# Sliding attention and the filters of the long convolutions in one block, in a two-layer mixer kernel on one Trainium2 core

## The chip, the core and the metric

The kernel is one program on one core of a Trainium2 chip. The metric is the device time of a launch in microseconds, the median of several runs. All arithmetic is 32-bit floating point. The engines are named as the profile names them: PE (TensorE; PEld is its weight load), DVE (VectorE), ACT (ScalarE), POOL (GpSimd), SP (SyncE, which issues most DMAs). "mem" is the on-chip memory, "banks" are the eight PSUM banks of 512 words per partition.

## What is computed

Two layers over 512 tokens of width 1024, with 256 context tokens. The first layer mixes by a gated delta rule and a differential attention; the second, which the change touches, by a sliding-window attention (8 heads of 64, two key heads, blocks of 128 queries against up to three blocks of keys and the 256 context tokens) and by two long convolutions with learned filters:

```python
def mixer_cd(hx, hz, w_in, w_out, sink, hy_conv, ...):
    qx, kx, vx, ux = split_cols(hx @ w_in, CD_SPLITS)
    qx = rope2d(...); kx = rope2d(...)
    ocx = swa_latent(qx, kx, vx, kz, vz, sink)
    odx = hyena(ux, hy_conv, hyena_filters(n, hy_w1, ...), hy_bias)
    out_x = jnp.concatenate([ocx, odx], axis=-1) @ w_out

def hyena_filters(n, w1, b1, w2, b2, w3, freq):
    h = jnp.sin(freq[0] * (feats @ w1 + b1))
    h = jnp.sin(freq[1] * (h @ w2 + b2))
    h = (h @ w3).reshape(n, 2, 2, 512) * jnp.exp(-t * deltas)
    kern = concatenate([h[:, :, 0], zeros, flip(h[1:, :, 1])])
    kern = kern * rsqrt(sum(kern * kern, axis=0) + EPS)
    return rfft(kern)

def hyena(u, conv_w, kf, bias):
    v, x1, x2 = jnp.split(dwconv(u, conv_w), 3, axis=-1)
    z = v
    for o, gate in enumerate((x1, x2)):
        z = gate * (fft_long_conv(z, kf[:, o]) + z * bias[o])
    return z
```

Each layer ends with an output projection, a norm and a feed-forward part.

## The kernel before, in words

The program is a row of stages. A stage is one block with a hand-written order of instructions for each engine; semaphores order them inside the block, and the next block begins when all engines have left this one. Weights come in slices of 1 MB or less through a ring of four buffers (`Core.stream`, `prefetch`, `issue`); SP issues a slice when its buffer has been read.

The stages around the change, in order:

- `down_and_project` (L1914): the down projection of the first feed-forward part; beside it POOL issues, one after the other, 24 slices of `w_mod` (`Down.load_side`, L1796) which PE multiplies after every second unit (L304); then the projections `swa_q` (4 tiles), `hy_in` (12 tiles, a three-tap convolution on ACT and DVE), `swa_k`, and the values. A tile is eight matmuls of 128x512 (L1865). At its end SP also loads the four slices of `cd_out`, the weights of the output projection after the mixing.
- `window_attention` (L2583): 32 units (4 query blocks x 8 heads). For a unit PE makes scores on one half of its rows (L2620, L2621, L2623), DVE adds window masks (L2691, L2693), takes the maximum (L2694) and forms the bias of the exponential (L2697), ACT takes the exponential (L2667) and that of the sink (L2669), DVE sums, inverts and scales (L2704 to L2706), PE turns the probabilities (L2633), ACT keeps them (L2660), and for two heads at once PE multiplies with the values (L2645), which DVE copies out (L2712). A score area is 512 or 640 wide, and there are two of them. POOL does nothing.
- `hyena` (L2991), a row of blocks: `turn_tiles` (L2747) turns eight tiles to token order; `filter_features` (L2783) loads all tables and makes the two sine layers; then for each of the two orders `filter_lags` (L2838: 8 products with `w3`, decay on DVE, squares on ACT summed over all tokens by PE with a matrix of ones, L2853), `transform` (L2902) of the filter with a scaling by the norm (L3014), `transform` of the signal with the complex product, shared between DVE (`product_c`, `join_s`) and POOL (`product_s`, L3033 to L3037), and `inverse` (L2960). After the first order four tiles are turned back. A transform is 16 matmuls of 128x512 (L2918), each two records in the trace; DVE unfolds its halves (L2931, L2932).
- `mix_and_up` (L1391: output projection), and the rest of the feed-forward part.

## Time and profile before

| | |
|---|---|
| median of 3 runs | 2686.13 us (2685.66 to 2688.75) |
| the profiled execution's own time | 2678.73 us |
| its span, first to last instruction | 2676.9 us |
| PE busy / DVE / ACT / POOL | 89% / 34% / 20% / 9% |
| granted PE clock, mean | 0.953 |

The profile is of one execution, read on its one core. Times in its rows are microseconds from the start of the span unless marked ns. A share of busy time is an average over stages that have different limits, so what counts for a stage is which chain of waits ends last in it. PEclk is the granted clock of PE as a share of 2.4 GHz.

### The profile page before, as it was taken

What the parts mean: (1) busy time and instruction counts of PE and PEld (TensorE: products, weight loads), DVE (VectorE), ACT (ScalarE), POOL (GpSimd) and SP (SyncE); (2) the same over time, 40 slices, a digit from 0 to 9 for tenths busy, and PEclk for the clock granted to TensorE, in tenths of its full rate; (3) what the DMA queues carried; (4) which work ended last, traced back from release to release, by engine and by line L of the source; (5) the groups of instructions that cost most, each with busy time, mean ns of one, the idle gap of its engine ahead of it and who ended that gap; (6) DMA issues with size and microseconds to landing.
All of it is one profiled execution on the core that took longest, in us unless ns stands there. A gap on an engine that the chain in (4) does not pass through costs nothing. (4 is left out here: it accounts for less than half of the span.)

```text
span 2676.9 us, 37700 instructions
## 1 busy us (share of the span) xinstructions
PE 2390.0 (89%) x16488; PEld 1631.4 (61%) x16488; DVE 899.2 (34%) x1717; ACT 537.4 (20%) x1252; POOL 232.4 (9%) x293
## 2 busy tenths in 40 slices
PE   4999899779958999999999999998667599999998
PEld 2566555468856755555569997456423385444798
DVE  2225602277732322222210032317555533222111
ACT  2104601421203311111110021115311031111110
POOL 1000100047720000000000000000020200000000
PEclk9999899889988999999999999998888799999999
DMA  8340010000030111111115566120100011221354
GB/s 304 132 158 26 1 47 16 0 2 4 4 128 1 63 39 56 63 32 63 53 58 164 164 192 207 48 77 2 60 0 0 0 63 63 71 86 63 97 144 139
DMA packets 190785, 193.46 MB, mean 72 GB/s; under 512 B 4970, under 2 KB 174622, under 8 KB 190430
## 3 DMA queue, kind: packets, MB, share of 16 engines
q1 hardware_dynamic: 177950, 145.55, 17.9%
q0 software_dynamic: 11584, 42.24, 4.4%
q8 instruction: 130, 2.13, 0.3%
q10 hardware_dynamic: 1088, 3.26, 0.3%
q14 instruction: 33, 0.27, 0.0%
HBM read 188.94 MB, written 2.10 MB: 71 GB/s over the span
## 5 line engine op out<-in xcount | busy, mean ns | idle before, releaser
L1446 PE MATMUL banks<-mem 128*128 128x512 f32 x1312 | 618.1, 591 | 0.0
L1780 PE MATMUL banks<-mem 128*128 128x128 f32 x3520 | 404.3, 277 | 11.2 <-PEq L1369 9.9
L1780 PEld LDWEIGHTS banks<-mem 128*128 128x128 f32 x3520 | 399.7, 193 | 21.2 <-issue 19.9
L461 DVE SCALAR_TENSOR_TENSOR mem<-banks,mem 128x511 f32<-128x511 f32 (+1 forms) x168 | 106.1, 660 | 748.5 <-ACT mem L1517 325.3
L1446 PEld LDWEIGHTS banks<-mem 128*128 128x128 f32 x1312 | 247.8, 189 | 172.0 <-issue 153.2
L1449 PEld LDWEIGHTS banks<-mem 128*128 128x128 f32 x672 | 127.1, 189 | 161.9 <-issue 161.9
L1449 PE MATMUL banks<-mem 128*128 128x256 f32 x672 | 200.1, 378 | 0.0
L1865 PE MATMUL banks<-mem 128*128 128x512 f32 x400 | 188.6, 602 | 6.0 <-issue 6.0
L1515 ACT ACTIVATE mem<-banks,mem 128x512 f32<-128x512 f32 x88 | 60.6, 689 | 628.3 <-PE banks L1449 373.5
L1391 PE MATMUL banks<-mem 128*128 128x256 f32 x640 | 144.4, 386 | 13.3 <-PEq L715 11.1
L917 PE MATMUL banks<-mem 64*64 64x64 f32 x3840 | 128.8, 221 | 18.5 <-DVE mem L1193 11.4
L1391 PEld LDWEIGHTS banks<-mem 128*128 128x128 f32 x640 | 123.3, 194 | 32.5 <-issue 14.0
L917 PEld LDWEIGHTS banks<-mem 64*64 64x64 f32 x3840 | 121.2, 137 | 28.7 <-DVE mem L1193 13.7
L398 PE MATMUL banks<-mem 128*128 128x512 f32 x256 | 130.9, 592 | 2.5 <-PEq L514 1.2
L1807 DVE COPY mem<-banks 128x128 f32<-128x128 f32 x40 | 11.7, 293 | 351.0 <-PE banks L1780 350.9
L1865 PEld LDWEIGHTS banks<-mem 128*128 128x128 f32 x400 | 75.3, 191 | 74.4 <-issue 70.8
L465 DVE SCALAR_TENSOR_TENSOR mem<-banks,mem 128x511 f32<-128x511 f32 (+1 forms) x168 | 105.8, 658 | 4.0
L1796 POOL DMA_DIRECT2D mem<-in_w_mod x24 | 17.3, 723 | 856.1 <-POOLq L1369 610.8
L401 PEld LDWEIGHTS banks<-mem 128*128 128x128 f32 x256 | 48.4, 189 | 61.7 <-issue 61.7
L1801 ACT ACTIVATE mem<-banks 128x128 f32<-128x128 f32 x40 | 11.1, 278 | 361.1 <-PE banks L1780 349.0
L2918 PE MATMUL banks<-mem 128*128 128x512 f32 x128 | 62.8, 653 | 17.0 <-PEq L2843 6.1
L401 PE MATMUL banks<-mem 128*128 128x256 f32 x256 | 76.2, 378 | 0.0
(306 smaller groups left out, 2641.0 us busy)
## 6 DMA issues: line engine op xcount, KB each, us to landing
mem<-in_ffn_w_up SPq DMA_DIRECT2D x44, 1024.0 KB, 5.4
mem<-in_ffn_w_down SPq DMA_DIRECT2D x64, 704.0 KB, 6.5
mem<-in_w_mod POOLq DMA_DIRECT2D x40, 1024.0 KB, 7.5
mem<-in_ab_w_in SPq DMA_DIRECT2D x14, 1024.0 KB, 5.3
mem<-in_w_mod SPq DMA_DIRECT2D x8, 1024.0 KB, 14.8
mem<-in_cd_w_in SPq DMA_DIRECT2D x8, 1024.0 KB, 5.3
mem<-in_ab_w_out SPq DMA_DIRECT2D x4, 1024.0 KB, 9.2
mem<-in_cd_w_out SPq DMA_DIRECT2D x4, 1024.0 KB, 5.1
```

What stands on the lines that cost most here:

```text
L398: last = nc.tensor.matmul(c.ps[:, 2 * (n % slots), :], w[:, k, :], ht[:, k, 0:N_X], start=k == 0, stop=k == KT - 1)
L401: last = nc.tensor.matmul(c.ps[:, 2 * (n % slots) + 1, 0:z], w[:, k, :], ht[:, k, N_X:N_X + z], start=k == 0, stop=k == KT - 1)
L461: step = v.scalar_tensor_tensor(out[:, 1:n], src[:, 0:n - 1], tap(0), out[:, 1:n], ALU.mult, ALU.add)
L465: step = v.scalar_tensor_tensor(out[:, 0:n - 1], src[:, 1:n], tap(2), out[:, 0:n - 1], ALU.mult, ALU.add)
L917: last = mm(c.ps[pa, LEVEL[i], fr], lhs[pa, fr], rhs[pa, fr], start=True, stop=True)
L1391: last = nc.tensor.matmul(c.ps[:, unit_banks[n % 4], 0:256], src[:, k, t * 128:(t + 1) * 128], w[:, k, :], start=k == 0, stop=k == KT - 1)
L1446: last = nc.tensor.matmul(c.ps[:, bank, :], w[:, k, :], ht[:, k, 0:N_X], start=k == 0, stop=k == KT - 1)
L1449: last = nc.tensor.matmul(c.ps[:, bank + 1, 0:z], w[:, k, :], ht[:, k, N_X:N_ALL], start=k == 0, stop=k == KT - 1)
L1515: f(dst[:, 0:N_X], c.ps[:, bank, :], ACT.Identity, scale=middle_tap(n, half)).then_inc(drained, 1)
L1780: last = c.nc.tensor.matmul(c.ps[:, n % self.n_banks, 0:128], hidden[:, k, t * 128:(t + 1) * 128], w, start=k == 0, stop=k == FT - 1)
L1865: last = c.nc.tensor.matmul(c.ps[:, self.bank(n)[0], :], w[:, k, :], ht[:, k, 0:N_X], start=k == 0, stop=k == KT - 1)
L2918: last = nc.tensor.matmul(c.ps[:, 4 * f + 2 * s + odd, :], hy.fwd[:, s, 2 * odd + t, f * 128:(f + 1) * 128], src(s)[:, 2 * odd + t, :], st ...
```

## The change

It does five things.

1. `down_and_project` also makes the filter features (the two sine layers) in its `hy_in` part: POOL issues six small loads ahead of the `w_mod` slices, PE makes one 33- and one 64-row matmul after tiles 5 and 8, DVE six operations after each, ACT one sine after each. Its SP no longer loads `cd_out`; that is now done by the convolution block once the last spectrum is formed.
2. Attention goes by pairs of heads: the scores of the two heads of a pair are issued in turns on the two row halves of PE, into one pair of score areas; two turns and one product with values for a pair. DVE does both maxima, then both weighings, of a pair.
3. In the same block all filter work is done in 16 steps, one for each pair: for each order four steps of lags (two products, kept by ACT, decayed, combined and accumulated by POOL with six operations, squared by ACT) and four steps of transform (four matmuls, kept by ACT, unfolded by POOL with two operations). The sum over tokens is taken once for each order at the end, from sums that POOL accumulated. Tables are loaded by SP at the start of the block.
4. The filters are no longer scaled by their norm; the norm is applied after the inverse transforms.
5. Turning, both convolutions and both gates are one block, `convolutions`; the inverse is in two halves, and the first half of it may run while DVE is at the second half of the product.

```diff
-        for n in range(self.issued, min(hi + ahead, len(self.loads))):
+        for n in range(self.issued, min(hi + ahead, self.range_of["cd_out"][0] if hi < self.range_of["cd_out"][1] else len(self.loads))):
...
+    net = FilterFeatures(c, Hyena(c), sem, 7)
...
-                c.stream(sp, name)
+                c.stream(sp, name, 0 if name == "swa_v" else RING)
...
+            net.load(pool)
             down.load_side(pool)
...
+                if n in (5, 8):
+                    net.multiply(pe, (n - 5) // 3)
...
+                if n in (6, 9):
+                    net.sine(act, (n - 6) // 3)
...
+                if n in (5, 8):
+                    net.reduce(dve, (n - 5) // 3)
...
+class Filters:
...
+    def load(self, eng):
+        hy, a = self.hy, self.c.a
+        eng.dma_start(hy.w3, a["hy_w3"][0]).then_inc(self.came, 16)
+        eng.dma_start(hy.decay, a["t_decay"].rearrange("(t p) n -> p t n", p=128)).then_inc(self.came, 16)
+        for s in range(2):
+            eng.dma_start(hy.fwd[:, s], a["t_fwd"][s].rearrange("(t p) n -> p t n", p=128)).then_inc(self.came, 16)
+        eng.dma_start(hy.bias0, a["hy_bias"][0, 0].partition_broadcast(128)).then_inc(self.came, 16)
...
+    def multiply(self, pe, n, part):
...
+        if n == 0 and part == 0:
+            pe.wait_ge(self.came, self.LOADED)
+        if n:
+            pe.wait_ge(self.kept, 2 * (n - 1) + part + 1)
+        if lag:
+            t, col = n % 8, (order * 2 + part) * 512
+            last = c.nc.tensor.matmul(out, hy.h2[:, t * 128:(t + 1) * 128], hy.w3[:, col:col + 512], start=True, stop=True)
+        else:
+            f, s = (n % 8 - 4) // 2, n % 2
+            if (f, s, part) == (0, 0, 0):
+                pe.wait_ge(self.ready, 8 * (order + 1))
+            for t in range(2):
+                last = c.nc.tensor.matmul(out, hy.fwd[:, s, 2 * part + t, f * 128:(f + 1) * 128],
+                                          hy.lags[:, s, 2 * part + t, :], start=t == 0, stop=t == 1)
...
+    def keep(self, act, n):
...
+        for part in range(2):
+            act.wait_ge(self.product, 2 * n + part + 1)
+            if n >= 2 and part == 0:
+                self.after(act, n - 2)
...
+    def after(self, eng, n):
...
+        if lag:
+            eng.wait_ge(self.ready, 2 * (lags + 1))
+            eng.wait_ge(self.squared, 2 * (lags + 1))
+        else:
+            eng.wait_ge(self.unfolded, 2 * (4 * (n // 8) + n % 8 - 4 + 1))
+    def square(self, act, n):
+        lags, lag = self.lag_step(n)
+        if lag:
+            for part in range(2):
+                act.wait_ge(self.decayed, 2 * lags + part + 1)
+                if lags:
+                    act.wait_ge(self.added, 2 * (lags - 1) + part + 1)
+                self.c.nc.scalar.activation(self.hy.lag_sq[part], self.hy.lag_raw[2 * (n % 2) + part], ACT.Square)\
+                    .then_inc(self.squared, 1)
+    def weigh(self, pool, n):
...
+            raw = [hy.lag_raw[2 * (n % 2) + part] for part in range(2)]
+            for part in range(2):
+                pool.wait_ge(self.kept, 2 * n + part + 1)
+                g.tensor_tensor(raw[part], raw[part], hy.decay[:, t, :], ALU.mult).then_inc(self.decayed, 1)
+            pool.wait_ge(self.decayed, 2 * lags + 2)
+            if order and t == 0:
+                pool.wait_ge(self.product, 16)
+            g.tensor_tensor(hy.lags[:, 0, t, :], raw[0], raw[1], ALU.add).then_inc(self.ready, 1)
+            g.tensor_tensor(hy.lags[:, 1, t, :], raw[0], raw[1], ALU.subtract).then_inc(self.ready, 1)
+            for part in range(2):
+                pool.wait_ge(self.squared, 2 * lags + part + 1)
+                if part or t:
+                    pool.wait_ge(self.added, 2 * lags + part)
+                    ins = g.tensor_tensor(hy.acc[order], hy.acc[order], hy.lag_sq[part], ALU.add)
+                else:
+                    ins = g.tensor_copy(hy.acc[order], hy.lag_sq[part])
+                ins.then_inc(self.added, 1)
+        else:
+            f, s = (n % 8 - 4) // 2, n % 2
+            total, mirrored, odd = hy.kern[order][:, s, f], hy.kern[order][:, s, 2 + f], hy.lag_raw[2 * (n % 2) + 1]
+            pool.wait_ge(self.kept, 2 * n + 2)
+            g.tensor_tensor(mirrored, *((odd, total) if s else (total, odd)), ALU.subtract).then_inc(self.unfolded, 1)
+            pool.wait_ge(self.unfolded, 2 * (4 * order + n % 8 - 4) + 1)
+            g.tensor_tensor(total, total, odd, ALU.add).then_inc(self.unfolded, 1)
...
+            def scores(p):
+                q, hp = pairs[p]
+                if p:
+                    pe.wait_ge(exped, 2 * p)
...
+                for hh, k0, k1, at in parts:
+                    pa = slice(64 * hh, 64 * hh + 64)
...
+            for i in range(n_pairs + 2):
+                if i < n_pairs:
+                    scores(i)
+                if 0 <= i - 2:
+                    values(i - 2)
+                if 0 <= i - 1 < n_pairs:
+                    turn_unit(2 * i - 2)
+                    filters.multiply(pe, i - 1, 0)
+                    turn_unit(2 * i - 1)
+                    filters.multiply(pe, i - 1, 1)
+            filters.norm_multiply(pe)
...
+            for i in range(n_pairs + 2):
+                if 0 <= i - 2:
+                    filters.keep(act, i - 2)
+                if 0 <= i - 3:
+                    filters.square(act, i - 3)
+                if 0 <= i - 1 < n_pairs:
+                    turned_copy(2 * i - 2)
+                if i < n_pairs:
+                    exps(2 * i)
+                    exps(2 * i + 1)
+                if 0 <= i - 1 < n_pairs:
+                    turned_copy(2 * i - 1)
...
+            for i in range(n_pairs + 2):
+                if i < n_pairs:
+                    maximum(2 * i)
+                    maximum(2 * i + 1)
+                    weigh(2 * i)
+                    weigh(2 * i + 1)
...
+def convolutions(c):
...
+            sp.wait_ge(spec_done, 4)
+            c.prefetch(sp, "cd_out")
...
+            for order in range(2):
+                forward(order, 0)
+                if order == 0:
+                    pe.wait_ge(v_act, 4)
+                    pe.wait_ge(v_dve, 4)
+                forward(order, 1)
+                if order == 0:
+                    pe.wait_ge(back_in, 32)
+                backward(order, 0)
+                if order:
+                    pe.wait_ge(unfolded, 8)
+                    for k in range(4):
+                        for t in range(4):
+                            last = nc.tensor.transpose(c.ps[:, bank(1, 1) + k, t * 128:(t + 1) * 128], hy.v[:, t, k * 128:(k + 1) * 128],
+                                                       c.tab["ident"])
+                        last.then_inc(z_turned, 1)
+                backward(order, 1)
...
+            def multiply(order, f):
+                g = 2 * order + f
+                kern = lambda s, mirror: hy.kern[order][:, s, 2 * mirror + f, :]
+                for s in range(2):
+                    dve.wait_ge(product, 4 * g + 2 + s + 1)
+                    dve.wait_ge(even_out, 2 * g + s + 1)
+                    total, mirrored, odd = z(s, 0), z(s, 1), c.ps[:, bank(order, f) + 2 * s + 1, :]
+                    v.tensor_tensor(mirrored, *((odd, total) if s else (total, odd)), ALU.subtract)
+                    v.tensor_tensor(total, total, odd, ALU.add).then_inc(unfolded, 1)
+                dve.wait_ge(unfolded, 2 * g + 2)
+                for mirror, total in enumerate((one, other)):
+                    v.tensor_tensor(total, z(0, mirror), kern(0, mirror), ALU.mult)
+                    link(v.tensor_tensor(part, z(1, mirror), kern(1, mirror), ALU.mult))
+                    link(v.tensor_tensor(total, total, part, ALU.subtract))
+                if order and f == 0:
+                    dve.wait_ge(inverse, 4)
+                v.tensor_tensor(hy.spec[:, 0, f, :], one, other, ALU.add)
+                v.tensor_tensor(hy.spec[:, 0, 2 + f, :], one, other, ALU.subtract).then_inc(spec_c, 1)
+                dve.wait_ge(spec_s, g + 1)
+                link(v.tensor_tensor(other_s, other_s, other_part_s, ALU.add))
+                v.tensor_tensor(hy.spec[:, 1, f, :], one_s, other_s, ALU.subtract)
+                v.tensor_tensor(hy.spec[:, 1, 2 + f, :], one_s, other_s, ALU.add).then_inc(spec_done, 1)
+                dve.wait_ge(spec_done, g + 1)
             for f in range(2):
+                multiply(0, f)
+            for t in range(4):
+                dve.wait_ge(inverse, t + 1)
+                link(v.tensor_tensor(one, c.ps[:, t, :], hy.root0, ALU.mult))
+                dve.wait_ge(weighted, t + 1)
+                link(v.tensor_tensor(one, one, hy.vb[:, t, :], ALU.add))
+                v.tensor_tensor(hy.v[:, t, :], one, hy.x1[:, t, :], ALU.mult).then_inc(gated, 1)
+                dve.wait_ge(gated, t + 1)
             for f in range(2):
+                multiply(1, f)
...
-def window_attention(c):
...
-def hyena(c):
...
-    window_attention(c)
-    hyena(c)
+    attention_and_filters(c)
+    convolutions(c)
```

## Rows read from the trace of the kernel before

**Rows 1.** The page's first line: the span.

```profile
span 2676.9 us, 37700 instructions
```

**Rows 2.** Stretches: us, busy PE, PEld, DVE, ACT, POOL, clock, DMA share, GB/s.

```profile
1803.60:1906.30 102.70, 82.28 (x593) 61.00 (x593) 74.10 (x229) 54.04 (x129) 0.01 (x1) 0.90 0.04 11
1906.30:2135.90 229.60, 144.10 (x340) 67.12 (x340) 126.02 (x162) 33.19 (x49) 35.72 (x24) 0.78 0.06 18
...
1929.70:1953.60 23.90, 20.84 (x32) 7.42 (x33) 10.91 (x16) 8.85 (x12) 0.00 (x0) 0.75 0.00 1
```

**Rows 3.** Timeline, one 640-wide attention unit: start, us, engine, line, operation.

```profile
1872.77 0.30 DVE L2691 TENSOR_TENSOR banks<-banks,mem 128x128 f32<-128x128 f32 x1 [0.69 <-PE banks L2623]
...
1874.55 0.80 ACT L2667 ACTIVATE mem<-banks,mem 128x640 f32<-128x640 f32 x1 [0.38 <-DVE mem L2697]
...
1874.82 0.56 DVE L2706 TENSOR_SCALAR mem<-mem 128x640 f32<-128x640 f32 x1
...
1875.29 0.29 DVE L2712 COPY mem<-banks 128x128 f32<-128x128 f32 x1
1875.34 0.28 ACT L2669 ACTIVATE mem<-mem 128x1 f32<-128x1 f32 x1
```

**Rows 4.** Timeline of PE: first scores, turns, values, scores on two row halves, transforms.

```profile
1810.62 1.23 PE L2620 MATMUL banks<-mem 64*128 64x256 f32 x4 [7.83 <-DVE mem L2681]
...
1863.45 0.77 PE L2633 MATMUL banks<-mem 128*128 128x128 f32 x5 [0.71 <-DVE mem L2706]
...
1864.15 1.32 PE L2645 MATMUL banks<-mem 128*64 128x128 f32 x20
...
251.52 1.89 PE L537 MATMUL banks<-mem 64*128 64x512 f32 x8
...
1954.55 13.06 PE L2918 MATMUL banks<-mem 128*128 128x512 f32 x30
...
1973.60 16.82 PE L2918 MATMUL banks<-mem 128*128 128x512 f32 x32 [5.99 <-PEq L224]
```

**Rows 5.** Four lines of code: duration ns min/median/max, first and last start.

```profile
L1141 POOL TENSOR_TENSOR mem<-mem x12: 1035/1043/1052, 598.0 to 767.6; 128x512 f32<-128x512 f32 x12
...
L3034 POOL TENSOR_TENSOR mem<-mem x4: 1704/1708/1712, 1987.4 to 2106.0; 128x512 f32<-128x512 f32 x4
...
L3014 DVE TENSOR_TENSOR mem<-mem x16: 684/690/695, 1962.8 to 2076.0; 128x512 f32<-128x512 f32 x16
...
L3024 DVE TENSOR_TENSOR mem<-mem x8: 1746/1750/1756, 1986.2 to 2109.8; 128x512 f32<-128x512 f32 x8
```

**Rows 6.** Timeline of the convolutions: turns, table load, product halves, gate, last inverse.

```profile
1906.30 4.08 PE L2760 MATMUL banks<-mem 128*128 128x128 f32 x32 [0.66 <-PEq L2598]
...
1951.19 1.28 ACT L2899 ACT_TABLE_LOAD   x1
...
1984.89 0.68 DVE L2932 TENSOR_TENSOR mem<-mem,banks 128x512 f32<-128x512 f32 x1
...
1997.35 0.69 DVE L3042 TENSOR_TENSOR mem<-mem 128x512 f32<-128x512 f32 x1
...
1998.77 0.69 DVE L2931 TENSOR_TENSOR mem<-mem,banks 128x512 f32<-128x512 f32 x1 [0.74 <-ACT mem L2949]
...
2013.03 0.69 DVE L3042 TENSOR_TENSOR mem<-mem 128x512 f32<-128x512 f32 x1
...
2022.64 0.69 DVE L3047 TENSOR_TENSOR mem<-mem 128x512 f32<-128x512 f32 x1 [1.36 <-PE banks L2977]
...
2116.95 16.87 PE L2979 MATMUL banks<-mem 128*128 128x256 f32 x64 [23.61 <-PEq L2908]
```

**Rows 7.** Timeline at the start of `down_and_project`, and a row of DMA issues.

```profile
1379.46 0.77 POOL L1796 DMA_DIRECT2D mem<-in_w_mod  x1 [610.82 <-POOLq L1369]
...
1392.13 1.04 PE L304 MATMUL banks<-mem 128*2 128x256 f32 x16
...
mem<-in_cd_w_out SPq DMA_DIRECT2D x4, 1024.0 KB, 5.1
```

More of the change, by code:

```diff
@@ new lines, in exps @@
+            def exps(u):
+                p, hh = u // 2, u % 2
+                n = cols(p)
+                act.wait_ge(maxed, 2 * p + 2)
+                if u >= 4:
+                    act.wait_ge(turned_ps, u - 3)
+                    act.wait_ge(weighed, u - 3)
+                nc.scalar.activation(prob[:, u % 4, 0:n], score(p, hh), ACT.Exp, bias=neg[:, u % 4:u % 4 + 1],
+                                     scale=scale, accum_out=total[:, u % 4:u % 4 + 1]).then_inc(exped, 1)
+                h = 2 * pairs[p][1] + hh
+                nc.scalar.activation(sink_exp[:, u % 4:u % 4 + 1], sink[:, h:h + 1], ACT.Exp,
+                                     bias=neg[:, u % 4:u % 4 + 1]).then_inc(sink_exped, 1)
@@ L2672, in _ @@
+            filters.norm(act)
+        @block.gpsimd
+        def _(pool):
+            for n in range(Filters.STEPS):
+                filters.weigh(pool, n)
         @block.vector
@@ new lines, in forward @@
+            def forward(order, f):
+                for odd in range(2):
+                    if f == 0:
+                        if order:
+                            pe.wait_ge(gated, 2 * odd + 2)
+                        else:
+                            pe.wait_ge(v_act, 2)
+                            pe.wait_ge(v_dve, 2)
+                    for s in range(2):
+                        for t in range(2):
+                            last = nc.tensor.matmul(c.ps[:, bank(order, f) + 2 * s + odd, :], hy.fwd[:, s, 2 * odd + t, f * 128:(f + 1) * 128],
+                                                    hy.v[:, 2 * odd + t, :], start=t == 0, stop=t == 1)
+                        last.then_inc(product, 1)
@@ new lines, in backward @@
+            def backward(order, f):
+                pe.wait_ge(spec_done, 2 * order + f + 1)
+                for i in range(4):
+                    cut = slice(i * 128, (i + 1) * 128)
+                    if order == 0:
+                        parts = [(i // 2, f)]
+                    else:
+                        parts = [(0, 1), (1, 0), (1, 1)] if f else [(0, 0)]
+                    for odd, half in parts:
+                        tokens = slice(256 * odd, 256 * odd + 256)
+                        for s in range(2):
+                            table, spec = hy.back[:, s, half, :], hy.spec[:, s, 2 * odd + half, :]
+                            flags = dict(start=(half, s) == (0, 0), stop=(half, s) == (1, 1))
+                            if order == 0:
+                                last = nc.tensor.matmul(c.ps[:, bank(order, 0) + i, :], table[:, cut], spec, **flags)
+                            else:
+                                last = nc.tensor.matmul(c.ps[:, bank(order, 0) + i, tokens], spec[:, cut], table[:, tokens], **flags)
+                    if f:
+                        last.then_inc(inverse, 1)
@@ L2763, in _ @@
         @block.scalar
         def _(act):
[L2765 to L2775 removed]
+            copy = lambda dst, src: nc.scalar.activation(dst, src, ACT.Copy)
@@ new lines, in _ @@
+            for n in range(0, 8, 2):
+                act.wait_ge(turned, n + 1)
+                copy((hy.v, hy.x1)[n // 4][:, n % 4, :], c.ps[:, n, :]).then_inc(v_act, 1)
+            for order in range(2):
+                for f in range(2):
+                    g = 2 * order + f
+                    if g:
+                        act.wait_ge(spec_c, g)
+                        act.wait_ge(spec_s, g)
+                    for s in range(2):
+                        act.wait_ge(product, 4 * g + s + 1)
+                        copy(z(s, 0), c.ps[:, bank(order, f) + 2 * s, :]).then_inc(even_out, 1)
@@ L2902, in transform @@
-def transform(c, src, hy, values, finish, finish_pool=None, join=None):
-    nc = c.nc
-    st, sem = stage(c)
-    with st, nc.Block() as block:
-        product, chained, pool_chained = sem("product"), sem("chained"), sem("pool_chained")
-        even_out, unfolded, finished, pool_finished = sem("even_out"), sem("unfolded"), sem("finished"), sem("pool_finished")
-        @block.tensor
-        def _(pe):
-            for f in range(2):
-                for s in range(2):
-                    for odd in range(2):
-                        for t in range(2):
-                            last = nc.tensor.matmul(c.ps[:, 4 * f + 2 * s + odd, :],
-                                                    hy.fwd[:, s, 2 * odd + t, f * 128:(f + 1) * 128],
-                                                    src(s)[:, 2 * odd + t, :], start=t == 0, stop=t == 1)
-                    last.then_inc(product, 1)
+            link = chain(pool, pool_chained)
```

610 lines of the change are left out of this document (258 added, 352 removed).

## The prediction

> **What bounds the kernel now.** I read the profiled execution's span first [rows 1], then the stretches of the two stages that the change rewrites [rows 2], then their timelines [rows 3, 4, 6]. Its own time is 2678.7 us, 7.4 us below the median of the runs; the sum is made on it and put on the median at the end. Attention takes 102.7 us, from 1803.6 to 1906.3, the convolutions 229.6 us, to 2135.9 [rows 2]. Neither is at the pace of a full engine: in the convolutions PE is busy for 144.1 us and DVE for 126.0, one after the other, and the granted clock is 0.78. There PE waits for DVE: each half of a complex product takes DVE 15 us (first unfold of the second half at 1998.77, last join at 2013.03 + 0.69 [rows 6]), and PE restarts at the low one of its two clocks (1.2 and 2.4 GHz). A transform of 32 records takes 30 in 13.06 us, 0.435 each, when warm, and 32 in 16.82 from cold: 2.8 us more [rows 4]. In attention it is the chain scores, maximum, exponential, weighing, turn, with PE busy for 82.3 of 102.7 us, and POOL idle.
>
> **Projection: +2.7 us.** Two matmuls of 512 columns in a stretch where PE is full: 2 x 2 x 0.435 = 1.7. DVE's six operations and ACT's sine lie beside the next tile (8 matmuls, 7 us), with a table load. POOL issues six small loads ahead of the first `w_mod` slice. Bounds: nothing, or 6 x 0.77 = 4.6, since PE first needs a slice at 1392.13, 12.7 us after its issue [rows 7]; I take 1. SP no longer moves `cd_out` here.
>
> **Convolutions: 229.6 becomes 103.** What goes: the features, the lags of both orders (23.9 for the first [rows 2]) and the filter's transforms. What stays, as a chain from the block's start:
> - turns 4.1 [rows 6]; the first forward transform, 8 matmuls at 0.87 and a few at the low clock: 13.5; unfolding then ends at 15.0. The rest of a half takes 1997.35 + 0.69 - 1985.57 = 12.5 [rows 6]: 27.5;
> - the second half, 15.0 with the copies of ACT beside DVE: 42.5. The second forward and the first inverse half lie under it;
> - the inverse's second half: first tile after 2 matmuls at the low clock, 3.5, then four gates of three chained operations like L3047's 0.69, 2.2 each: 55.0. This was 8 matmuls more per order, then a block of turns;
> - the half of a forward transform that waits for the last gate, 1.7 and unfold: 59.8; + 12.5 + 15.0 = 87.3. The turns of z lie under it;
> - the last inverse: 24 of the former 32 matmuls. 32 took 16.87 [rows 6], 8 warm ones fewer take 3.4 less: 101; two DVE operations and the block's end: 103.
> The `cd_out` slices are issued at 87.3 and land 5.1 us later in the quiet median [rows 7]; PE needs the first at 103, the fourth some 20 us after. Cost nothing under that cover of 16 us; without it up to 5 us.
> Gain 126.6. Bounds: 95 (no cold restarts, ACT and DVE steps overlap better) and 112 (each of the four waits costs one more restart of 2.8).
>
> **Attention with the filter steps: 102.7 becomes 158.** This is the uncertain term. Terms for a pair:
> - PE: scores on two row halves. L537 does that for 2 x 768 columns in a span of 1.89 us, where at 0.87 for 512 columns they would take 2.6 one after the other [rows 4]; by columns 2 x 640 is 1.5, 2 x 512 1.15. Values 1.32, turns 2 x 0.66 [rows 4], lag matmuls 2 x 0.87, transform matmuls 4 x 0.87. With gaps: transform step 8.1 us (640 wide) or 7.3 (512).
> - DVE: a unit takes 1875.29 - 1872.77 = 2.5 [rows 3], a pair with its copy 5.25, and DVE now waits between maxima and weighings for ACT's first exponential and sink, 1874.55 to 1875.62 [rows 3], 1.2 with hops: 6.5, or 5.4 at 512.
> - POOL: six operations of 512 in a lag step, two in a transform step. Alone one takes 1.04 us (L1141); beside DVE's operations with two inputs from mem 1.71 (L3034), and DVE's own go from 0.69 (L3014) to 1.75 (L3024) [rows 5]: the sum of both durations. DVE's weighing has such an operation (L2704) and L2706, whose 0.56 for 640 elements [rows 3] is quicker than L3014's 0.69 for 512, so it uses more than one path; no row shows it beside POOL. Its bounds are no wait and 1.04. I take 1.2 us a unit for both: a lag pair on DVE is 8.6 at 640 and 7.7 at 512. POOL loses 1.5 to DVE: 8.0 for six.
> The Trainium skill, "SBUF — State Buffer", section "Who interferes with whom", says that the shared port pair is locked for a whole instruction, two-input operations and `tensor_scalar` in its two-port mode among them. The trace agrees for two inputs; L2704 and L2706 would each wait up to one POOL operation.
>
> Order of time from the stage's start. First scores at 1810.62 - 1803.6 = 7.0, as before [rows 4]. PE ends pair 0's turns and first lag step at 20.6, at the low clock. Lags 1 to 3 run at 7.8, 7.8, 8.3: 44.5. Then PE's queue meets `ready`, the wait that the change adds: transform step 4 needs all four lags. POOL gets the last pair of lags only after ACT's keep, and before them the two additions for the step before, which wait for ACT's squares: 1.7 + 6 x 1.04 + contention 1 = 9 us after PE began pair 5: 53.5; behind that wait stand the turn of the pair's second head and so everything. The rest of that pair 4.5 + 1 cold, three transform pairs 24.3: 83.3. Pair 9 at 7.3 and lags of order two at 8.6, 8.6, 8.0: 115.8. The second wait 9: 124.8; 5.5; two pairs 14.6; the last without scores 6: 151. The sum of squares, `Ln`, a table load of 1.28 [rows 6] and `Exp`, with the last unfolding: 6.5. In all 157.5, +55.
> Bounds: no contention, lag steps at 6.9 and 5.8 (the chain score-maximum-exponential), the two waits 8: 143, +40. Every POOL operation at 1.71: lag step 10.5, the waits 12.5: 178, +75.
>
> **Sum.** -126.6 + 55 + 2.7 = -69: 2678.7 becomes 2610, and 2617 on the scale of the median.
>
> **The rivals.**
> 1. Light contention: attention +40, total 2602. For it: L1141's 12 runs, over 170 us of another stage, are all within 1.035 and 1.052 [rows 5], though DVE worked there too. Against: L3034's 1.71. 0.22.
> 2. Full contention, every POOL operation at 1.71 and DVE held for a whole one at each of its own: attention +75, total 2638. For it: rows 5, where both ran densely. Against: of a unit's eight DVE operations only L2704 and L2706 are of that sort, the others have an input in PSUM or one element. 0.20. That is what the Trainium skill's lock rule (same page and section) gives if POOL is never idle; the trace shows it only for equal lengths.
> 3. The scores of the two heads run one after the other, 2.1 instead of 1.5, and PE, not DVE, is the bound in all pairs: 16 x 0.6 + 6 = +16, total 2633. Against: L537's 1.89. 0.08.
> 4. Slower than before: in-order queues leave nothing of a filter step beside its pair. PE's product n waits for ACT's keep n-1, ACT's square for POOL's decay, POOL's addition for ACT's square. A lag step then costs 6.9 + 1.7 + ACT's four operations of 512, each under L2667's 0.80, 2.5 + 6 x 1.71 = 21.4, a transform step 8.1 + 1.7 + 3.4 = 13: 8 x 21.4 + 8 x 13 + 14 = 289, +187, total about 2750. It decides from an attention stage above 226 us. Against: each wait looks back one or two steps, and two kept areas alternate. 0.02.
> 5. A better overlap than forecast of both stages (convolutions 95, attention +35): 2588. 0.06.
>
> **How the numbers follow.** The forecast has 0.42. The time is its own, 2617. The range takes in rivals 1 to 3 and the bounds of the convolutions: low 2617 - 15 - 8 - 9 = 2585, high 2638 + 9 + 3 = 2650. A difference of 0.2% (5 us) is about what a measurement of this kernel can tell. All cases but rival 4 are far beyond it: faster 0.97, same 0.01, slower 0.02.
>
> **What would show it.** In the profile after: a stretch of attention of some 158 us with POOL busy for over 70, the scaling longer than L2706's 0.56 when POOL runs, PE idle twice for about 5 us behind POOL at the first transform matmul of each order; convolutions of 103 us in four product halves of 15; DMA not on the chain at the output projection. Wrong would be: lag pairs no slower than transform pairs (rival 1), POOL operations all near 1.7 (rival 2), score matmuls of 2 us a pair (rival 3).

## The result and the profile after

The changed kernel takes 2606.26 us, the median of 4 runs (2604.04 to 2607.28); the kernel before, beside it on the same chip, 2687.28 (2685.66 to 2688.75). The ratio is 0.9698, interval [0.9681, 0.9714]: 81 us faster, where 69 were forecast (2617). The profiled execution took 2604.04 us.

The page, then the two rewritten stretches (us, busy PE, PEld, DVE, ACT, POOL, clock, DMA share, GB/s), which answer to [rows 1, 2]:

```profile
span 2602.2 us, 37620 instructions
...
1808.30:1961.70 153.40, 120.70 (x698) 73.12 (x699) 91.17 (x229) 79.91 (x183) 79.80 (x64) 0.84 0.07 20
1961.70:2063.20 101.50, 71.76 (x209) 41.34 (x209) 75.55 (x84) 9.39 (x16) 38.48 (x24) 0.85 0.16 52
```

| | before | after | change | forecast |
|---|---|---|---|---|
| projection ends at | 1803.6 | 1808.3 | +4.7 | +2.7 |
| attention (after: with all filter work) | 102.7 | 153.4 | +50.7 | +55 |
| convolutions | 229.6 | 101.5 | -128.1 | -126.6 |
| the rest of the span | 541.0 | 539.0 | -2.0 | 0 |
| span | 2676.9 | 2602.2 | -74.7 | -69 |

The other 6 us of the 81 stand in no stage of these two traces: before's profiled execution lay 8.6 us under the median given here, after's 2.2 under its own.

The timeline of PE in attention (start, us, engine, line): a lag pair of 512 columns, the two waits for POOL, and three scores of transform pairs with 640 columns:

```profile
1833.82 1.13 PE L2870 MATMUL banks<-mem 64*128 64x256 f32 x8
...
1839.27 1.39 PE L2870 MATMUL banks<-mem 64*128 64x128 f32 x12
...
1860.87 3.75 PE L2723 MATMUL banks<-mem 128*128 128x512 f32 x4 [4.08 <-POOL mem L2782]
...
1867.83 1.36 PE L2870 MATMUL banks<-mem 64*128 64x256 f32 x12
...
1875.06 1.36 PE L2870 MATMUL banks<-mem 64*128 64x256 f32 x12
...
1882.33 1.36 PE L2870 MATMUL banks<-mem 64*128 64x256 f32 x12
...
1930.60 3.75 PE L2723 MATMUL banks<-mem 128*128 128x512 f32 x4 [6.39 <-POOL mem L2782]
```

The first such wait ended 52.6 us after the stage's start (forecast 53.5), the second 122.3 (124.8), and what was left took 31.1 (32.7). A transform pair takes 7.2 us, not 8.1.

What single DVE and POOL operations take in the same stage (ns minimum/median/maximum): the addition of the sink's exponential, the scaling, the negated maximum, the reciprocal, POOL's decay:

```profile
L2979 DVE TENSOR_TENSOR mem<-mem x32: 146/159/1220, 1819.3 to 1948.9; 128x1 f32<-128x1 f32 x32
...
L2981 DVE TENSOR_SCALAR mem<-mem x32: 486/556/1452, 1819.7 to 1949.3; 128x512 f32<-128x512 f32 x16, 128x640 f32<-128x640 f32 x16
...
L2974 DVE TENSOR_SCALAR mem<-mem x32: 214/214/216, 1816.9 to 1946.8; 128x1 f32<-128x1 f32 x32
...
L2980 DVE RECIPROCAL mem<-mem x32: 162/164/167, 1819.5 to 1949.1; 128x1 f32<-128x1 f32 x32
...
L2777 POOL TENSOR_TENSOR mem<-mem x16: 1258/1270/1280, 1827.6 to 1926.6; 128x512 f32<-128x512 f32 x16
```

An addition of one element for each partition takes up to 1.22 us, about one POOL operation long. The scaling is held in the same way, the other two never. Here is how it looks in the pair that begins at 1839.27 (DVE and POOL take turns, then PE has waited 3.06 us for DVE):

```profile
1839.49 1.26 DVE L2981 TENSOR_SCALAR mem<-mem 128x512 f32<-128x512 f32 x1
1840.55 1.32 POOL L2781 TENSOR_TENSOR mem<-mem 128x512 f32<-128x512 f32 x1
1840.67 1.22 DVE L2979 TENSOR_TENSOR mem<-mem 128x1 f32<-128x1 f32 x1
1841.84 1.25 POOL L2782 TENSOR_TENSOR mem<-mem 128x512 f32<-128x512 f32 x1
...
1842.13 1.26 DVE L2981 TENSOR_SCALAR mem<-mem 128x512 f32<-128x512 f32 x1
...
1843.73 1.97 PE L2895 MATMUL banks<-mem 128*64 128x128 f32 x16 [3.06 <-DVE mem L2998]
```

Over the whole stage the groups of these two lines show it (busy us, mean ns):

```profile
L2981 DVE TENSOR_SCALAR mem<-mem 128x512 f32<-128x512 f32 (+1 forms) x32 | 23.8, 745 | 1.1
L2979 DVE TENSOR_TENSOR mem<-mem 128x1 f32<-128x1 f32 x32 | 13.5, 422 | 19.8 <-ACT mem L2925 19.7
```

### The profile page after: what moved, and what is told of

Its sections match the earlier page's. It is cut to its first block and busy times, and to the rows that moved or that the text cites. A ratio compares the mean times of both kernels' runs of the same rounds, so it can differ in the third digit from the quotient of the medians.

```text
span 2602.2 us, 37620 instructions
## 1 busy us (share of the span) xinstructions
PE 2358.5 (91%) x16466; PEld 1618.3 (62%) x16466; DVE 871.6 (33%) x1651; ACT 542.5 (21%) x1276; POOL 318.3 (12%) x363
## 3 DMA queue, kind: packets, MB, share of 16 engines
q10 hardware_dynamic: 1088, 3.26, 0.3%
## 5 line engine op out<-in xcount | busy, mean ns | idle before, releaser
L1446 PE MATMUL banks<-mem 128*128 128x512 f32 x1312 | 618.1, 591 | 0.0
L1865 PE MATMUL banks<-mem 128*128 128x512 f32 x400 | 191.4, 609 | 6.0 <-issue 6.0
L917 PE MATMUL banks<-mem 64*64 64x64 f32 x3840 | 128.0, 221 | 18.6 <-DVE mem L1193 11.4
L398 PE MATMUL banks<-mem 128*128 128x512 f32 x256 | 130.9, 592 | 2.5 <-PEq L514 1.2
L304 PE MATMUL banks<-mem 128*2 128x256 f32 x768 | 54.9, 413 | 23.5 <-DMA mem<-in_w_mod 23.5
(318 smaller groups left out, 2687.7 us busy)
```

Of the source, the lines that this page charges most:

```text
L304: last = c.nc.tensor.matmul(c.ps[32 * g:32 * g + 2, bank, 0:256], c.sc[:, k, :], w[:, kk, 256 * g:256 * g + 256], start=k == 0, stop=k == ...
L398: last = nc.tensor.matmul(c.ps[:, 2 * (n % slots), :], w[:, k, :], ht[:, k, 0:N_X], start=k == 0, stop=k == KT - 1)
L917: last = mm(c.ps[pa, LEVEL[i], fr], lhs[pa, fr], rhs[pa, fr], start=True, stop=True)
L1446: last = nc.tensor.matmul(c.ps[:, bank, :], w[:, k, :], ht[:, k, 0:N_X], start=k == 0, stop=k == KT - 1)
L1865: last = c.nc.tensor.matmul(c.ps[:, self.bank(n)[0], :], w[:, k, :], ht[:, k, 0:N_X], start=k == 0, stop=k == KT - 1)
```

## The experiments

All times of a stage below are from the profiled execution of that kernel: attention from 5.2 us before the first scores (that is the projection's end after the change) to the first turns of the convolutions, the convolutions from there to the first matmul of the output projection. The projection ended between 1808.3 and 1816 in these executions, though no edit touches anything ahead of it; so totals of kernels with one run are not compared, only their stages. The a runs, the b runs and the c and d runs were made on three chips, each beside the kernel before, whose median was 2687.4, 2691.3 and 2687.7 us; the column "of before" is the ratio to it, and a total on the chip of the b runs has to be read by that column.

| kernel | total, median (range) | of before | attention | convolutions |
|---|---|---|---|---|
| changed | 2606.3 (2604.0 to 2607.3) | 0.9698 | 153.4 | 101.5 |
| a1, attention alone | 2572.5, one run | | 119.1 | |
| a2, no POOL in the filter steps | 2578.7, one run | | 125.4 | |
| b2, no sums of squares | 2597.8, one run | | 143.7 | |
| a3, scores head by head | 2611.9 (2610.3 to 2614.0) | 0.9720 | 156.8 | |
| b1, waits by part | 2598.9 (2596.1 to 2603.2) | 0.9661 | 143.7 | |
| b3, addition as `tensor_scalar` | 2606.5 (2596.5 to 2607.7) | 0.9680 | 149.6 | |
| a4, products on DVE | 2600.3 (2599.1 to 2603.0) | 0.9677 | 153.6 | 94.9 |
| b4 = a4 + b1 + b3 | 2591.1 (2588.0 to 2595.5) | 0.9627 | 140.7 | 96.0 |
| d1, late loads | 2611.9 (2610.3 to 2614.6) | 0.9725 | 153.1 | 105.2 |
| c1, one head at a time | 2634.2 (2630.0 to 2638.4) | 0.9801 | 178.5 | |
| c2 = c1 + b1 + a4 | 2610.6 (2593.5 to 2615.0) | 0.9705 | 148.4 | 96.3 |

The 95% intervals of the ratios are 0.0026 to 0.0054 wide. That of b1 ([0.9647, 0.9675]) and that of b4 lie wholly below the changed kernel's, that of c1 above it; those of a3, a4, b3 and d1 overlap with it, and what is said of these four rests on their stages.

**What the 50.7 us of attention are made of: a1, a2, b2.**

a1:

```diff
-                    filters.multiply(pe, i - 1, 0)
-                    filters.multiply(pe, i - 1, 1)
...
-                    filters.keep(act, i - 2)
-                    filters.square(act, i - 3)
...
-                filters.weigh(pool, n)
```

> Leaves out all filter steps of the attention block (TensorE's lags and transforms, ScalarE's keeps and squares, GpSimd's operations, the norm); the roots are set to 1 instead. Attention by pairs is all that is left of the 153.4 us. Theory A (the pair's own chain scores, two maxima, exponentials, next scores sets the pace, and the filter steps are the rest): two pairs without blocked VectorE operations took 5.9 and 5.45 us with 512 columns; with 640 columns some 6.4; 8 x 5.5 + 8 x 6.4 + 5 at the start + 6 at the end = 106 us, as long as the 102.7 of one head at a time, so the change by itself buys nothing in attention. Theory B (pairs on row halves are themselves quicker): 90 us or less. Theory C (the filter steps lie beside and only late waits cost): over 130.

119.1 us: no theory's number. The stage of pairs with nothing beside them is 16.4 us longer than that of one head at a time [rows 2]; from the first scores on it is 18.2 (113.9 for 95.7), since the first scores now come 5.2 us after the stage's start and not 7.0. The timeline of a1 shows why:

```profile
1870.40 1.36 PE L2870 MATMUL banks<-mem 64*128 64x256 f32 x12 [1.70 <-ACT mem L2920]
...
1873.40 0.22 DVE L2969 TENSOR_SCALAR mem<-mem 128x1 f32<-128x1 f32 x1
...
1875.05 0.21 DVE L2969 TENSOR_SCALAR mem<-mem 128x1 f32<-128x1 f32 x1
1875.30 0.80 ACT L2920 ACTIVATE mem<-banks,mem 128x640 f32<-128x640 f32 x1 [0.68 <-DVE mem L2969]
...
1876.27 0.78 ACT L2920 ACTIVATE mem<-banks,mem 128x640 f32<-128x640 f32 x1
...
1877.19 1.36 PE L2870 MATMUL banks<-mem 64*128 64x256 f32 x12 [1.70 <-ACT mem L2920]
```

The next pair's scores go into the same areas and wait for both exponentials, and the first exponential waits until both maxima are taken (`act.wait_ge(maxed, 2 * p + 2)`): scores, two maxima, two exponentials, 6.8 us round with PE idle for 1.7 of it. The kernel before had a score area for each of two heads, and two heads took 6.0 us:

```profile
1865.40 0.70 PE L2620 MATMUL banks<-mem 64*128 64x256 f32 x2
...
1871.38 0.70 PE L2620 MATMUL banks<-mem 64*128 64x256 f32 x2
```

At 512 columns a pair takes 5.5 in a1 and two heads took 4.9 before. That makes 8 x 0.8 + 8 x 0.6 = 11 us of the 18, an estimate from rounds at the high clock. The rest was not separated; the clock is part of it (from 1830 to 1850 a1 was granted 0.75, the kernel before 1.00). Whether an earlier first exponential would shorten the round no run tests.

a2 keeps the filter steps' work on PE and ACT (ACT's waits for POOL go as well, and the first transform matmul waits only for POOL's start):

```diff
         @block.gpsimd
         def _(pool):
-            for n in range(Filters.STEPS):
-                filters.weigh(pool, n)
...
             if (f, s, part) == (0, 0, 0):
-                pe.wait_ge(self.ready, 8 * (order + 1))
+                pe.wait_ge(self.ready, 3)
```

> Leaves out GpSimd's operations of the filter steps (decay, sum, difference, sums of squares, unfolding); TensorE's and ScalarE's stay, so the filters are wrong. Theory A (GpSimd blocks VectorE and is late at the transforms, which is most of the price): attention about 120 us of 153.4, no 1.2 us operations at the additions and scalings. Theory B (TensorE in order, with its cold stretches, is the price): 140 us or more, GpSimd or not.

125.4 us, as theory A had it; no operation of DVE is long any more (the scaling 16.7 us in all, as before the change, the addition 5.1). So PE's and ACT's filter work costs 6.3 us and POOL's 28.0. The clock moves with them: PE is busy for 71.9 us in a1 and for 109.2 in a2, yet the stage is only 6.3 longer, at a mean granted clock of 0.92 instead of 0.85; with POOL's operations it is 0.84.

b2 takes 2.5 of 7.6 us from each lag step of POOL, by leaving out the sums (the waits for them go too; POOL still waits for ACT's squares):

```diff
-                if part or t:
-                    pool.wait_ge(self.added, 2 * lags + part)
-                    ins = g.tensor_tensor(hy.acc[order], hy.acc[order], hy.lag_sq[part], ALU.add)
-                else:
-                    ins = g.tensor_copy(hy.acc[order], hy.lag_sq[part])
-                ins.then_inc(self.added, 1)
+                if t == 0 and part == 0:
+                    g.tensor_copy(hy.acc[order], hy.lag_sq[part]).then_inc(self.added, 1)
```

> Leaves out the sums of the squares on GpSimd but for a copy (so the filters' norms are wrong): a lag step of GpSimd is 5.1 instead of 7.6 us, shorter than a pair. Without any GpSimd work attention took 125.4 us instead of 153.4. If those 28 us are lateness at the transforms in the main, they go nearly whole here: attention 130 us. If blocked VectorE operations are the main part, they shrink with GpSimd's busy time (80 us to 62): 137 us or more, with both waits gone.

143.7, 9.7 less, and neither version of the theory: both waits stayed. The waits, POOL's last lag step ahead of the first of them, then the scaling and the addition in b2:

```profile
PE banks L2723 <- POOL mem L2782: 9.5, 2, 4.8
```

```profile
1853.76 2.49 POOL L2777 TENSOR_TENSOR mem<-mem 128x512 f32<-128x512 f32 x2 [3.26 <-ACT mem L2764]
```

```profile
L2977 DVE TENSOR_SCALAR mem<-mem 128x512 f32<-128x512 f32 (+1 forms) x32 | 20.1, 627 | 1.1
L2975 DVE TENSOR_TENSOR mem<-mem 128x1 f32<-128x1 f32 x32 | 8.8, 274 | 19.9 <-ACT mem L2921 19.9
```

The waits went from 10.5 to 9.5 us, so in the main they are not the sums that POOL had still to do: they are the length of one passage from the last lag product through ACT's keep and POOL's four operations (here 1849.2 to 1858.9, of which POOL stood idle for 3.26 until ACT's squares of the step before were done), while PE meets the transform one pair later. In the changed kernel POOL's two sums fill that idle time. The held time of the two DVE lines fell from 15.5 to 7.1 us over their undisturbed 21.8, by 8.4. These two, 9.4, are close to the 9.7, but that held DVE time goes to the stage's time one for one is not shown by it: the mean clock rose at the same time, from 0.84 to 0.89. In the same way POOL's 28.0 are 10.5 of waits, 15.5 of held DVE operations, and low clock behind both, without a share that these runs settle. The first transform products behind the two waits took 3.75 us each instead of 1.88 in a2, and the pair of the rows above, with four DVE operations held by 3.1 us together (the three shown and one more addition), took 10.5 us where a2's took 6.8.

**The waits: b1.**

```diff
-            if (f, s, part) == (0, 0, 0):
-                pe.wait_ge(self.ready, 8 * (order + 1))
+            if f == 0:
+                pe.wait_ge(self.ready, 8 * order + 4 * part + 3 + s)
```

> The transform matmuls of each order wait only for the lag tiles that they read (of the first part: the first two tiles) instead of for all of the order's. Theory A (GpSimd's last lag step is late there and TensorE, in order, holds turns and scores back; waits of 4.1 and 6.4 us): the part 0 matmuls fill the wait, the next scores start 4.0 and 4.5 us earlier: 8 us faster. Rival (the pace is set elsewhere, TensorE's idle time is only moved): within 2 us.

7.4 us faster in the medians, 9.9 by the ratios, 9.7 in the stage. The two waits fell from 10.5 to 2.5 us together. In b1's timeline of PE the first part runs at once, the turn behind it too, and 1.0 us is left of the first wait:

```profile
1856.23 1.88 PE L2723 MATMUL banks<-mem 128*128 128x512 f32 x4
1857.96 0.71 PE L2883 MATMUL banks<-mem 128*128 128x128 f32 x5
1859.66 1.96 PE L2723 MATMUL banks<-mem 128*128 128x512 f32 x4 [1.00 <-POOL mem L2781]
```

The part 0 matmuls also take 1.88 us instead of 3.75: without the wait PE is at its high clock there.

**Does sparing one operation from POOL help: b3.**

```diff
-                link(v.tensor_tensor(total[:, b], total[:, b], sink_exp[:, b], ALU.add))
+                link(v.tensor_scalar(total[:, b], total[:, b], sink_exp[:, b], None, ALU.add))
```

> The addition of the sink to the sum (128x1) as a tensor_scalar with the sink as its scalar, as the 128x1 tensor_scalar of the maximum, which took 0.21 us in all 32 cases, instead of a tensor_tensor, which took 0.16 to 1.22. Theory A (it is not blocked, but the scaling behind it, mem to mem over 128x512, then waits for the same GpSimd operation instead): the time within 2 us, the scaling's mean rises from 0.74 us. Theory B (the blocked time of the additions, 13.5 - 32 x 0.16 = 8.4 us, goes from the chain): 5 to 8 us faster.

The median is the same, 2606.5, but the kernel before was 4 us slower on that chip; by the ratios b3 is some 5 us faster (0.9680 against 0.9698, with overlapping intervals). The addition takes 0.21 us in all cases (6.8 in all). The scaling's mean did not rise, it is 720 ns. The stage is 3.8 us shorter, and the two waits are 15.3 us instead of 10.5: a pair that is through earlier meets POOL earlier. So theory A's reason was wrong, and between its total and theory B's the runs do not decide; of what the additions and scalings gave back, 7.5 us, the waits took 4.8. Beside b1's edit it is worth 3.0 us in the stage (b4's 140.7 for b1's 143.7; a4's edit lies behind it), and there too the waits grew, from 2.5 to 8.2.

**The three together: b4.** It was expected at 2591 us if the gains add (6, 8 and 1), and at 2599 if that of the filter steps came back as a later wait for POOL. The median is 2591.1. The agreement is partly luck, since the sum was made from medians of two chips; by the ratios b4 is 19 us below the changed kernel, and the three alone are 5.6, 9.9 and 4.8. Its attention is 12.7 us shorter and its convolutions 5.5.

**The row halves: a3.**

```diff
-                    parts = [(hh, k0, k1, at) for k0, k1, at in keys for hh in range(2)]
+                    parts = [(hh, k0, k1, at) for hh in range(2) for k0, k1, at in keys]
```

(and in the same way for 640 columns).

> The score matmuls of a pair one head after the other instead of alternating between the row halves. If the halves work at the same time (1.14 us for a pair of 512 columns where four single ones would be 2.1) and the scores are on the chain of each pair: 0.9 to 1.2 us for each of 16 pairs, less where a pair waits for GpSimd: 8 to 17 us slower. Rival (the alternation gives nothing, or scores are hidden behind VectorE): within 2 us.

5.6 us slower, between the two, and 3.4 in the stage. The score groups, of a3 with 512 and with 640 columns:

```profile
1837.68 1.13 PE L2870 MATMUL banks<-mem 64*128 64x256 f32 x8
...
1870.41 1.68 PE L2870 MATMUL banks<-mem 64*128 64x128 f32 x12
```

At 512 columns the order makes no difference (1.13 both), at 640 it costs 0.32. One head's scores alone took 1.3 us at 640 columns in the kernel before, so two heads in 1.68 still overlap: the halves work beside each other whichever order they are issued in, as long as both are at hand. Eight times 0.32 is 2.6 of the stage's 3.4 us; the other 2.2 of the 5.6 lie outside the stage.

**The convolutions: a4.**

```diff
-                    tt(one_s, z(0, 0), kern(1, 0), ALU.mult)
...
-                    tt(other_part_s, z(1, 1), kern(0, 1), ALU.mult).then_inc(spec_s, 1)
+                v.tensor_tensor(one_s, z(0, 0), kern(1, 0), ALU.mult)
...
+                v.tensor_tensor(other_part_s, z(1, 1), kern(0, 1), ALU.mult).then_inc(spec_s, 1)
```

(five operations of each half go from POOL to DVE).

> In the convolutions GpSimd's five products and sums of each half go to VectorE. Theory A (the two engines exclude each other on memory to memory operands: eleven operations took 9.0 us together, where VectorE alone starts one every 0.60 us): a half takes 20 x 0.60 = 12.1 us instead of 14.86, so 4 x 2.8 = 11 us faster. Theory B (GpSimd's work is beside VectorE's and takes it off): five more operations a half, 4 x 5 x 0.60 = 12 us slower.

6.0 us faster (ratio to before 0.9677 [0.9662, 0.9691], the changed kernel's 0.9698 [0.9681, 0.9714]), 6.6 in the stage. A half of the changed kernel, with both engines, from the second unfold's end on:

```profile
1990.33 0.69 DVE L3152 TENSOR_TENSOR mem<-mem 128x512 f32<-128x512 f32 x1
1990.38 1.77 POOL L3128 TENSOR_TENSOR mem<-mem 128x512 f32<-128x512 f32 x1 [6.40 <-DVE mem L3149]
1990.94 1.75 DVE L3153 TENSOR_TENSOR mem<-mem 128x512 f32<-128x512 f32 x1
1992.11 1.71 POOL L3129 TENSOR_TENSOR mem<-mem 128x512 f32<-128x512 f32 x1
1992.73 1.64 DVE L3154 TENSOR_TENSOR mem<-mem 128x512 f32<-128x512 f32 x1
```

and a4's, with DVE alone:

```profile
1989.32 0.69 DVE L3139 TENSOR_TENSOR mem<-mem 128x512 f32<-128x512 f32 x1
1989.93 0.69 DVE L3140 TENSOR_TENSOR mem<-mem 128x512 f32<-128x512 f32 x1
1990.65 0.69 DVE L3141 TENSOR_TENSOR mem<-mem 128x512 f32<-128x512 f32 x1
```

The two engines take turns, one operation each, and six of DVE's with five of POOL's last 9.0 us; alone DVE starts one every 0.60, or 0.72 where it waits for the one before. A half is 13.15 us with twenty operations instead of 14.86 with fifteen. Of the expected 11 us 7 came, because nine of the twenty wait for one before. For the lengths POOL has here, sharing such products with it loses. In attention, where POOL's operations of this sort take 1.27 us, the same move was not tried.

**The loads for the output projection: d1.**

```diff
-            sp.wait_ge(spec_done, 4)
+            sp.wait_ge(inverse, 8)
             c.prefetch(sp, "cd_out")
```

> The loads for the output projection are issued after the last inverse transform instead of at the fourth half's end, 12 us later. Theory A (they are hidden as they are and were on the path before): their landing, 9.2 us, less the 3.3 us of TensorE's own wait there, comes on the path: 5 to 9 us slower. Rival (hidden either way): within 2 us.

5.7 us slower, 3.7 in the stage. The four issues take 5.38 us from 2060.84, and the projection starts at 2067.87 instead of 2063.18:

```profile
2067.87 4.58 PE L1391 MATMUL banks<-mem 128*128 128x256 f32 x10 [7.06 <-PEq L224]
```

As the change has them they are hidden (issued at 2047.6, landing 9.2 us later, needed at 2063.2).

**One head at a time with the filter steps: c1, c2.** The loop of the kernel before, with half a filter step for each head and one PSUM bank each for the values and the filter products:

```diff
-            for i in range(n_pairs + 2):
-                if i < n_pairs:
-                    scores(i)
...
+            for i in range(n_units + 4):
...
+                    filters.multiply(pe, u // 2, u % 2)
```

> Attention one head at a time as in the kernel before (two score buffers), with the filter steps beside it half a step per head; the rest as in the changed kernel. Attention alone took 119.1 us by pairs and 102.7 by heads. Theory A (the pairs pay 16 us for having one score buffer, and TensorE's row halves give back less than that): TensorE would then set the pace, some 134 us without waits and 144 with the two at the transforms: 9 us faster than the changed kernel. Theory B (the pairs are what makes room on TensorE for the filter steps; one head's scores of 640 columns take 1.29 us, a pair's 1.36, so 20 us more on TensorE): 165 us or more in attention, 12 us or more slower.

And for c2:

> As the run before, with the transforms' waits by part (7.4 us in the pair form) and the convolutions' products on VectorE alone (6 us). If theory A holds and the gains add: 9 + 7 + 6 below 2606, 2584 us, and faster than the best so far (2591). If theory B holds: above 2600.

c1 is 28 us slower than the changed kernel, c2 20 slower than b4 (21 by the ratios), which differs from it by the form of the loop (and b3's edit). Theory A fell by its total, but not for theory B's reason alone. Up to the first transform both kernels run the same instructions in the same order; here are the same 20 us of c1 and of c2, in which c1 gets through 55 PE records and c2 through 99:

```profile
1830.00:1850.00 20.00, 20.00 (x55) 10.24 (x52) 10.46 (x25) 9.41 (x23) 8.28 (x8) 0.50 0.00 1
```

```profile
1830.00:1850.00 20.00, 17.95 (x99) 11.29 (x98) 17.65 (x39) 14.04 (x32) 16.59 (x14) 1.00 0.00 1
```

In c1 PE was busy without a gap from 1830 to 1870 and stayed at the low clock (0.50, 1.2 GHz); in c2 it had gone to the high one by 1825. c2's six runs lie at 2593.5 and 2597.1, and at 2607.6 to 2615.0; the profiled one is of the lower two, with attention at 148.4 where b1's pairs have 143.7. So the form by heads is 4.7 us slower even where the clock rose early; PE is busy for 131.1 us of it instead of 119.9. Both loops by heads also have one bank less for the filter products, which was not tested apart. That c2's four slower runs, up to 22 us behind, stayed at the low clock as c1 did is inferred from c1 and from their mean clocks (0.951 to 0.954, the two faster ones 0.960 and 0.962); none of them was profiled. The seven kernels by pairs with several runs spread over 3 to 11 us. Why the clock rises in one and not in the other no run here shows.

## Why the prediction was right, and where it was not

The forecast's own sum was 2610 for the profiled execution, which took 2604; its median 2617 became 2606, with before's profile 8.6 under its median and after's only 2.2. Point by point:

- **Projection, +2.7; measured +4.7.** The two products took 1.07 us each, so 2.1 instead of 1.7. The small loads cost nothing: PE's first slice was there at 1392.13 as before [rows 7]. 1.7 came from a low clock behind a turn (sixteen records at 1682.97 took 8.37 us, the same ones before 7.03), 0.85 from the stretches ahead. Such amounts vary from run to run by more than the term: the same code ended between 1808.3 and 1816 in the runs above.
- **Convolutions, 103; measured 101.5.** The chain held at its steps: gates' end 53.6 after the start (55.0), the four halves 14.86 each (15.0), the last inverse 98.2 (101). Turns took 5.5 instead of 4.1. That DVE and POOL gain nothing from sharing was in the profile of before already [rows 5], the sum of both durations, and I carried it along without asking what DVE alone would take (a4).
- **`cd_out` at no cost: right.** It lands in 9.2 us instead of 5.1 and has room for it (d1: 3.7 to 5.7 us without cover). Attention's first scores come 1.8 us earlier than forecast (5.2 for 7.0), since the load of the sink's values lands 2.7 us after its issue instead of 4.5; it no longer stands behind `cd_out`'s loads, which is the likely reason and was not tested.
- **Attention, 157.5; measured 153.4.** Total and both waits' ends within 4.1, 0.9 and 2.5 us, but the make-up was partly another, and that the parts came out so near is luck. The step "lag pair on DVE is 8.6 at 640 and 7.7 at 512", each with 1.2 us of contention a unit, is not what happens. Lag steps 1 to 3 were forecast at 7.8, 7.8 and 8.3, together 23.9; by the ends of their products they took 5.7, 5.8 and 12.2, together 23.7. Those of the second order, forecast at 8.6, 8.6 and 8.0, took 6.9, 6.9 and 11.4. The pairs are nearly free of contention until POOL has fallen behind; then two additions and two scalings of one pair are each held, and the pair takes over 10. Of the held 15.5 us 13.9 lie beside the eight lag steps, which makes 0.9 a unit there for the forecast's 1.2. POOL's operation is 1.27, not 1.04: L1141 was the wrong row, though the near one.
- **The pair form** was priced nearly right: 6.9 and 5.8 us for a pair without contention, 6.8 and 5.5 in a1. What the prediction never did was to set it beside the 6.0 and 4.9 us that two heads took before, so it did not say that the form alone costs 16.4 of the +50.7 (a1). The chances given to rival 3 went to the row halves, which work as forecast (1.13 for 1.15, 1.36 for 1.5).
- **Too high and too low.** Transform pairs took 7.2 us for the forecast 8.1, and contention was less. Too low was the low clock: the prediction gives it 1 us behind the first wait, where the rest of that pair took 7.0 us for the forecast 5.5, and nothing in the pairs with held operations (0.84 is the stage's mean clock, 0.92 without POOL's operations).
- **The waits at `ready`.** Placed right, and explained half right. I priced them by POOL's additions for the step before and six operations (9 us); the trace has these six, and 9.1 and 9.7 us from the last lag product to the wait's end. But b2 shows that they stay with the additions gone, since the passage through ACT and POOL is longer than a pair. I took the code's wait as the dependence; b1 shows that the first matmuls never needed it.
- **The rule of the Trainium skill** ("SBUF — State Buffer", "Who interferes with whom") that a shared port pair is locked for a whole instruction: rows L2979 and L2981 show it, up to 1.22 and 1.45 us, and the `tensor_reduce` and the operations with an input in PSUM were never held, as the Trainium skill says. Weighed as rival 2 it gave 178 us; measured are 153.4, with POOL busy for only 79.8 of them.

The better version is b4, 2591.1 us, 0.9627 [0.9614, 0.964] of the kernel before: 15 us below the changed kernel in the medians, 19 by the ratios.

## What to carry to other kernels

Before giving half of DVE's two-input work to POOL, add up what DVE would take alone: where the two exclude each other, the sum of both durations is the price, and a long operation of the slower engine can also hold a one-element operation of the faster one. A stage that is shared by two loops has a latency of its own from one to the other; let each matmul wait for the tiles that it reads, not for the group. When a loop is rewritten to make room for other work, time it empty too: here the new form lost 16 us that nobody asked for, and is ahead again only beside the filter steps (143.7 us for 148.4 by heads). And compare runs from several chips by their ratios to one kernel that ran on each.

## What the runs showed of the hardware that I had not expected

- A `tensor_tensor` of one element for each partition with both inputs in mem takes 0.15 to 1.22 us beside POOL; a `tensor_scalar` of the same size (0.21) and a reciprocal (0.16) are never held.
- The same POOL operation, 128x512 with two inputs in mem, takes 1.04 us in one stage [rows 5] and 1.27 in another with no DVE operation of that sort beside it. No run shows why.
- PE's clock can stay at 1.2 GHz through 40 us in which PE has no gap (c1, 1830 to 1870), while the same instruction stream is at 2.4 GHz in another execution (c2). The Trainium skill, "TensorE: Matmul & The Clock Gate", section "Part 1: The HAM clock gate (the "warmup" mystery)", calls the warm-up variable from run to run and its price under 1% of a typical span. The runs agree: c2's six differ by 21.5 us, 0.8% of the time.
- Two heads' score matmuls on the two row halves overlap as well when all of one head's are issued first (1.13 us both ways at 512 columns).
